# Attention weights in high and low parts for every second part of a row, and the output weights loaded in the mLSTM

## The chip, the core and the metric

The kernel runs on one core of a Trainium2 chip. Its engines are TensorE (PE, whose weight loads the profile lists apart as PEld), VectorE (DVE), ScalarE (ACT), GpSimd (POOL) and SyncE (SP), which here only issues DMAs. Each engine takes its instructions in order and waits for others by semaphores. The metric is the device time of one execution in microseconds.

## What is computed

One step of a one-layer encoder, for a prompt of 2048 tokens and a sample of 32 tokens with a past of 1024. Half of the mixing width is an mLSTM of 4 heads, half stick-breaking attention of 8 heads of 64; both go through one output projection, and a gated feed-forward net with a short convolution follows. The stages run one after the other: front (norm, input projection), attention, mLSTM, output projection, feed-forward up, feed-forward down.

```python
def stick_breaking_block(q, k, v, q_pos, k_pos):
    z = jnp.einsum('bhtd,bhsd->bhts', q, k).astype(jnp.float32) * (SB_DIM ** -0.5)
    mask = k_pos[None, :] < q_pos[:, None]
    log_beta = jnp.where(mask, jax.nn.log_sigmoid(z), -jnp.inf)
    log_1m = jnp.where(mask, jax.nn.log_sigmoid(-z), 0.0)
    rest = lax.cumsum(log_1m, axis=3, reverse=True) - log_1m
    a = jnp.exp(log_beta + rest)
    return jnp.einsum('bhts,bhsd->bhtd', a.astype(v.dtype), v)
...
    mix = jnp.concatenate([y_a, y_b], axis=-1) @ p['w_out']
    x = x + g1 * mix
```

## The kernel before

**Attention.** A row is a head h and a query block i of 128 tokens. It is cut into parts of up to four key blocks, last part first; such a part is an item (h, i, g), and a head has 40 of them: four rows of one item, four of two, four of three, four of four. In all there are 320 items of the prompt, 6 of the sample (ahead of head 3) and 10 that only turn past keys and queries. An item goes through the engines like this:

- PE multiplies queries and keys into a_z (L973; a mask product, L984, for a row's first item), which has NZ = 3 buffers. It waits there until ACT's second sigmoid of the item three before is done.
- ACT makes sigmoid(-z) into aB (L894) and sigmoid(z) into aS (L899, ring of 8).
- DVE runs the product along the row backwards into aC (L919).
- POOL multiplies aS by it (L957): these are the weights.
- PE turns them, 128 columns at a time, into a_x (L999, NX = 2 buffers).
- ACT (even items) or DVE (odd items) copies them into aA (L903, L886, ring of 4).
- PE multiplies weights and values in float32, one product of 128x64 a key block (L1015).
- DVE copies a finished row from a_out into aof (L934, ring of RO = 8), and SP stores it (L846).

The order is written out by hand: each engine walks `steps` and at step n does the operation for an item at a fixed distance (PE turns n-3, makes z of n+4 and the product of n-6; ACT makes the sigmoids of n+2, then copies n-4; DVE scans n, copies n-4, finishes n-7). So whoever waits holds up everything behind it on its engine.

SP loads queries and keys of head h+1 (six DMAs, L810) and its values (L828, av, two buffers) when the first row of head h is done, ahead of the store of that row; the loads of heads 0 and 1 stand at the start. In head 3 it also loads the whole of w_out (4 MB, L864), into the memory that the turned past keys have left.

**mLSTM.** A loop over 17 tiles of 128 tokens. SP loads ahead (three parts of the projections, a slice of w_ada for the modulation); ACT and POOL split w_out into high and low parts of the rounded format beside tiles 0 and 1 (L1141, L1128), four slices of 128x1024 each. The 16-record product of the modulation (L1266) closes each tile on PE.

**Output projection.** Per tile: loads (L1376 to L1378), norms on ACT and DVE, a turn on PE, a split of y, then three products each of 128x512 for (high, high), (low, high) and (high, low).

## Time and profile before

| | us |
|---|---|
| median of 3 runs (lowest, highest) | 3372.08 (3371.84, 3379.27) |
| the profiled execution | 3376.13 |
| its span on the core | 3374.5 |
| PE busy in it | 3177.0 (94%) |
| PEld, DVE, ACT, POOL busy | 2801.5, 1541.5, 1074.6, 757.8 |

Busy times are shares of the whole span and average over stages with different limits; which stage is bound by what is read from stretches of it. Attention lies between about 806 and 1345 us, the mLSTM from there to 1540, the output projection from 1540 to about 1778.

### The profile page before, as it was taken

The numbers are of one execution on the slowest core, as the hardware profiler recorded it, in microseconds if no ns is written. First come the engines' busy times: TensorE is split into PE (matmuls) and PEld (weight loads), VectorE is DVE, ScalarE is ACT, GpSimd is POOL, SyncE is SP. The second block draws the span as 40 slices with busy tenths as digits, with TensorE's granted clock in tenths as the row PEclk, the third lists the DMA queues.
The fourth block names the chain that finished last, engine by engine and source line by source line (L and its number), as shares of the span: only waits on it lengthen the run. The fifth ranks groups of instructions, "written<-read, shape, count | busy, mean of one in ns | idle before, by whom it ended". The sixth has DMA issues, their size and how long they took to land. (4 is left out here: it accounts for less than half of the span.)

```text
span 3374.5 us, 45756 instructions
## 1 busy us (share of the span) xinstructions
PE 3177.0 (94%) x17258; PEld 2801.5 (83%) x17258; DVE 1541.5 (46%) x1982; ACT 1074.6 (32%) x2063; POOL 757.8 (22%) x669
## 2 busy tenths in 40 slices
PE   7999998998999999896996999999999994999999
PEld 3878887777998998675886999999999994887886
DVE  1300025513887898674653544444344434234322
ACT  3611122213766776223553222122212212112111
POOL 3411113212665665200111111111111112002000
PEclk9999999998999999898997999999999997999999
DMA  5322224424423420564644111111111114335332
GB/s 185 113 67 69 75 79 129 137 90 118 112 52 101 95 56 12 187 217 146 194 150 150 51 50 50 50 34 42 50 50 50 50 38 152 140 121 174 139 136 70
DMA packets 249431, 335.88 MB, mean 100 GB/s; under 512 B 58380, under 2 KB 170440, under 8 KB 242508
## 3 DMA queue, kind: packets, MB, share of 16 engines
q1 hardware_dynamic: 233102, 284.75, 27.6%
q0 software_dynamic: 14864, 49.31, 4.3%
q8 instruction: 82, 1.34, 0.2%
q14 instruction: 51, 0.42, 0.0%
q10 hardware_dynamic: 1332, 0.06, 0.0%
HBM read 225.16 MB, written 108.89 MB: 99 GB/s over the span
## 5 line engine op out<-in xcount | busy, mean ns | idle before, releaser
L1774 PE MATMUL facc<-h2H,fwH 128*128 128x416 f32 x1760 | 617.5, 351 | 25.5 <-DVE h2L L1723 25.5
L1774 PE MATMUL facc<-h2L,fwH 128*128 128x416 f32 x1760 | 617.1, 351 | 0.0
L1774 PE MATMUL facc<-h2H,fwL 128*128 128x416 f32 x1760 | 617.0, 351 | 0.0
L642 PE MATMUL pacc<-pring,h1H 128*128 128x512 f32 x1360 | 444.3, 397 | 10.6 <-POOL h1L L524 5.8
L957 POOL TENSOR_TENSOR aS<-aS,aC 128x512 f32<-128x512 f32 (+3 forms) x326 | 333.7, 1029 | 203.1 <-DVE aC L919 200.3
L919 DVE TENSOR_TENSOR_SCAN aC<-aB,aC,a 128x512 f32<-128x512 f32 (+3 forms) x326 | 362.8, 1113 | 16.1 <-ACT aB L894 9.9
L1666 ACT ACTIVATE fU<-facc 128x416 f32<-128x416 f32 (+1 forms) x220 | 113.1, 514 | 787.5 <-PE facc L1774 787.5
L1740 DVE TENSOR_SCALAR fV<-fU,fcw,fcb 128x2048 f32<-128x2048 f32 x88 | 110.2, 1295 | 536.8 <-ACT fU L1668 536.7
L1774 PEld LDWEIGHTS facc<-h2H,fwH 128*128 128x128 f32 x1760 | 330.9, 188 | 28.8 <-issue 26.2
L1774 PEld LDWEIGHTS facc<-h2L,fwH 128*128 128x128 f32 x1760 | 331.0, 188 | 2.4
L1774 PEld LDWEIGHTS facc<-h2H,fwL 128*128 128x128 f32 x1760 | 330.8, 188 | 2.6
L1983 PE MATMUL dacc<-dwH,daH 128*128 128x512 f32 (+1 forms) x748 | 294.2, 393 | 37.0 <-POOL dwL L1850 24.5
L1710 POOL TENSOR_TENSOR fwL<-fraw,fwH 128x1024 fp32r<-128x1024 f32 x44 | 132.4, 3011 | 848.2 <-ACT fwH L1657 848.2
L642 PEld LDWEIGHTS pacc<-pring,h1H 128*128 128x128 f32 x1360 | 259.2, 191 | 66.2 <-POOL pring L520 6.9
L1015 PEld LDWEIGHTS a_out<-av,aA 128*128 128x128 f32 x2176 | 283.5, 192 | 19.3 <-issue 1.9
L1983 PE MATMUL dacc<-dwL,daH 128*128 128x512 f32 (+1 forms) x748 | 293.6, 393 | 0.0
L1983 PE MATMUL dacc<-dwH,daL 128*128 128x512 f32 (+1 forms) x748 | 293.6, 392 | 0.0
L1015 PE MATMUL a_out<-av,aA 128*128 128x64 f32 x2176 | 284.4, 270 | 0.0
L642 PE MATMUL pacc<-pring,h1L 128*128 128x512 f32 x680 | 267.6, 394 | 0.0
L973 PE MATMUL a_z<-ak,aq 128*128 128x512 f32 (+3 forms) x640 | 210.6, 411 | 13.2 <-DMA aq<-qk_T 13.2
L1923 ACT ACTIVATE daH<-da 128x2816 fp32r<-128x2816 f32 (+1 forms) x34 | 83.5, 2456 | 406.2 <-PE dacc L1983 350.3
L894 ACT ACTIVATE aB<-a_z 128x512 f32<-128x512 f32 (+3 forms) x326 | 174.4, 535 | 118.0 <-PE a_z L984 50.7
(261 smaller groups left out, 4773.7 us busy)
## 6 DMA issues: line engine op xcount, KB each, us to landing
da<-act_d SPq DMA_DIRECT2D x32, 1408.0 KB, 7.8
proj_out<-pstage SPq DMA_DIRECT2D x119, 256.0 KB, 2.0
fraw<-w_up SPq DMA_DIRECT2D x44, 512.0 KB, 5.7
act_d<-fV SPq DMA_DIRECT2D x22, 1024.0 KB, 5.3
qk_T<-pturn POOLq DMA_DIRECT2D x68, 256.0 KB, 3.1
mwa<-w_ada SPq DMA_DIRECT2D x16, 1024.0 KB, 5.4
praw<-w_in SPq DMA_DIRECT2D x56, 256.0 KB, 2.9
aq<-qk_T SPq DMA_DIRECT2D x28, 512.0 KB, 11.8
```

The lines of the kernel that those rows point to most:

```text
L642: op = mm_(acc[:, n % NB], h[:, kk, tok(t)], weight(q, w), start=(kk == 0 and part == 0), stop=(kk == KD - 1 and part == 2))
L894: nc.scalar.activation(part(B, RB, n), part(Z, NZ, n), ACT.Sigmoid, scale=-1.0).then_inc(pass_ready, 1)
L919: v.tensor_tensor_scan(buf[:, a:b][:, ::-1], part(B, RB, n)[:, ::-1], nought[:, 0:width(n)], buf[:, b:b + 1], ALU.mult, ALU.add).then_inc( ...
L957: nc.gpsimd.tensor_tensor(at, at, buf[:, a + 1:b + 1], ALU.mult).then_inc(w_ready, 1)
L973: mm = nc.tensor.matmul(to, Q[:, b, half, i * P:(i + 1) * P], K[:, b, span], start=(half == 0), stop=(half == 1), skip_group_check=True)
L1015: mm = nc.tensor.matmul(O[:, r % 2, 0:SD if kind == PROMPT else 4 * SD], weight[:, j * P:(j + 1) * P], value, start=(top(n) and j == 0), s ...
L1666: op = nc.scalar.activation(U[:, j, 2 + at:2 + end], acc[:, bank(q, w), 0:end - at], ACT.Copy)
L1710: nc.gpsimd.tensor_tensor(wL[:, j], raw[:, j], wH[:, j].bitcast(F32), ALU.subtract).then_inc(w_low, 1)
L1740: v.tensor_scalar(V[:, j, at:at + width], U[:, j, u0:u0 + width], tap(0), cb[:, ft], ALU.mult, ALU.add).then_inc(first_tap, 1)
L1774: mm = nc.tensor.matmul(dst, a[:, j, kk], h[:, kk, cols], start=(kk == 0 and m == 0), stop=(kk == KD - 1 and m == 2))
L1923: nc.scalar.activation(aH[:, i.b, :, 0:i.width], a[:, i.b, :, 0:i.width], ACT.Copy).then_inc(a_high, 1)
L1983: mm = nc.tensor.matmul(acc[0:w, i.b], l[:, i.b, kk, 0:w], m[:, kk], start=(kk == 0 and n == 0), stop=(kk == NF - 1 and n == 2))
```

## The change

1. Every second item of the prompt (the 160 of `in_two`, on 608 of the 1088 key blocks) is weighed in two parts. ACT copies the turned weights into AH, in the rounded format F32R; DVE subtracts that from a_x into AL. PE multiplies AH by the pair [high part, low part] of the values (128 columns), then AL by the high part (64 columns), both into the same row of a_out. DVE copies 128 columns of such a row into aot, and POOL adds the two halves nine items later (`add_parts`), before SP may store the row. 112 rows of 128 are of that kind.
2. ACT now copies every turned item, the others into A as before, and does so at the beginning of its step, ahead of the two sigmoids. DVE copies only the turned past keys. Each of the rings is two deep.
3. The values of head h+1 are split (ACT `split_values`, POOL a subtraction) at item (h, 8, 2), the thirteenth of head h; those of head 0 at its third item. ACT waits there for the load of these values.
4. The ring of finished rows, aof, is 4 deep, not 8.
5. w_out is loaded at the end of SP's list in the mLSTM instead of in head 3, and split at the start of the output projection: ACT all eight slices, POOL and DVE four subtractions each. The gate and norm rows are loaded ahead of the first tile there. The bias of the modulation has a buffer of its own.

```diff
+    in_two = set([n for n in scored if items[n][0] == PROMPT][1::2])
...
+    split_at = {scored[2]: 0}
+    split_at.update({items.index((PROMPT, h, NPT // 2, NPT // 2 // W4)): h + 1 for h in range(SH - 1)})
-    NZ, NX, RB, RS, RA, RC, RO = 3, 2, 4, 8, 4, 4, 8
+    NZ, NX, RB, RS, RA, RC, RO = 3, 2, 4, 8, 2, 4, 4
+    RT = 4
...
                 sp.wait_ge(o_taken, r + 1)
+                if r in rows_in_two:
+                    sp.wait_ge(o_summed, rows_in_two.index(r) + 1)
...
-                if kind == PROMPT and (h, i) == (3, 0):
-                    sp.wait_ge(turned, max(x for x in range(N) if items[x][0] in (KEYS, QUERIES)) + 1)
-                    sp.wait_ge(blank_stored, 16)
-                    sp.dma_start(w_out[:], d["w_out"].rearrange("(k p) n -> p k n", p=P)).then_inc(w_out_in, 16)
...
+                ring, order, done = (AH, two, high_ready) if n in in_two else (A, whole, taken[0])
+                if order[n] >= RA:
+                    act.wait_ge(av_done, rank[kept_by[n]] + 1)
+                to = ring[:, order[n] % RA, 0:width(n)]
+                nc.scalar.activation(to, X[:, n % NX, 0:width(n)], ACT.Copy).then_inc(done, 1)
...
+            def split_values(h):
+                b = h % 2
+                act.wait_ge(v_in[b], 16 * (h // 2 + 1))
+                nc.scalar.activation(V2[:, b, :, 0], V[:, b], ACT.Copy).then_inc(v_high, 1)
             for n in steps:
+                every(take, n - 4)
+                if n in split_at:
+                    split_values(split_at[n])
                 scores(passing, n + 2)
                 scores(stopping, n + 2)
-                every(take_even, n - 4)
...
+                elif n in in_two:
+                    dve.wait_ge(high_ready, two[n] + 1)
+                    at = two[n] % RA
+                    v.tensor_tensor(AL[:, at, 0:width(n)], X[:, n % NX, 0:width(n)], AH[:, at, 0:width(n)].bitcast(F32),
+                                    ALU.subtract).then_inc(taken[1], 1)
...
+            BEHIND = 9
+
+            def add_parts(n):
+                if not last(n) or row(n) not in rows_in_two:
+                    return
+                e, p = rows_in_two.index(row(n)), prompt_row(n)
+                pool.wait_ge(o_taken, row(n) + 1)
+                at_least(pool, stored[p % RO], 16 * (p // RO))
+                nc.gpsimd.tensor_tensor(of[:, p % RO], ot[:, e % RT, 0:SD], ot[:, e % RT, SD:], ALU.add).then_inc(o_summed, 1)
             for m, n in enumerate(scored):
...
                 nc.gpsimd.tensor_tensor(at, at, buf[:, a + 1:b + 1], ALU.mult).then_inc(w_ready, 1)
+                if n in split_at:
+                    e = split_at[n] % 2
+                    pool.wait_ge(v_high, split_at[n] + 1)
+                    nc.gpsimd.tensor_tensor(V2[:, e, :, 1], V[:, e], V2[:, e, :, 0].bitcast(F32), ALU.subtract
+                                            ).then_inc(v_low, 1)
+                if m >= BEHIND:
+                    add_parts(scored[m - BEHIND])
...
+                    if n in in_two:
+                        nc.tensor.matmul(out[:, 0:2 * SD], AH[:, two[n] % RA, cols],
+                                         V2[:, h % 2, b].rearrange("p s e -> p (s e)"), start=first, stop=False,
+                                         skip_group_check=True)
+                        mm = nc.tensor.matmul(out[:, 0:SD], AL[:, two[n] % RA, cols], V2[:, h % 2, b, 0], start=False,
+                                              stop=end, skip_group_check=True)
...
             tiles(sp, body)
+            sp.dma_start(w_out[:], d["w_out"].rearrange("(k p) n -> p k n", p=P)).then_inc(w_out_in, 16)
+            sp.wait_ge(w_out_in, 16)
             sp.wait_ge(mod_row, NPT)
```

How the rows of an engine stand is shown at three places. First ACT in head 5, where it comes to the ninth item (384 wide). Before:

```order
L894 ACTIVATE aB<-a_z 128x128
L899 ACTIVATE aS<-a_z 128x128
L903 ACTIVATE aA<-a_x 128x256
L894 ACTIVATE aB<-a_z 128x512
L899 ACTIVATE aS<-a_z 128x512
L894 ACTIVATE aB<-a_z 128x512
L899 ACTIVATE aS<-a_z 128x512
L903 ACTIVATE aA<-a_x 128x384
L894 ACTIVATE aB<-a_z 128x256
```

The same stretch after; `av<-av 128x16x64` is the split of the values of head 6, and aAH the high part of a_x:

```order
L917 ACTIVATE aA<-a_x 128x256
L890 ACTIVATE aB<-a_z 128x128
L895 ACTIVATE aS<-a_z 128x128
L917 ACTIVATE aAH<-a_x 128x512
L890 ACTIVATE aB<-a_z 128x512
L895 ACTIVATE aS<-a_z 128x512
L917 ACTIVATE aA<-a_x 128x384
L927 ACTIVATE av<-av 128x16x64
L890 ACTIVATE aB<-a_z 128x512
L895 ACTIVATE aS<-a_z 128x512
L917 ACTIVATE aAH<-a_x 128x512
```

The copy has moved ahead of the sigmoids of its step, there is one in each step, and the split stands between the copy of the ninth item and the sigmoids of the fifteenth.

Second POOL at the start of head 5, after; `aS<-aS,aC` is the product of L957, `aof<-aot` the addition of a row's two halves, of which the one behind the width of 384 belongs to the last row of head 4:

```order
L1006 TENSOR_TENSOR aS<-aS,aC 128x512
L1006 TENSOR_TENSOR aS<-aS,aC 128x256
L1006 TENSOR_TENSOR aS<-aS,aC 128x512
L1006 TENSOR_TENSOR aS<-aS,aC 128x384
L1000 TENSOR_TENSOR aof<-aot 128x64
L1006 TENSOR_TENSOR aS<-aS,aC 128x512 x2
L1000 TENSOR_TENSOR aof<-aot 128x64
L1006 TENSOR_TENSOR aS<-aS,aC 128x512
L1006 TENSOR_TENSOR aS<-aS,aC 128x128
L1010 TENSOR_TENSOR av<-av 128x16x64
L1000 TENSOR_TENSOR aof<-aot 128x64
```

Before, POOL's list holds only the products here. Third SP at the start of the output projection, before:

```order
L1376 DMA ey<-h_d 128x512
L1377 DMA ey<-o_rows 128x512
L1378 DMA eo<-proj_out 128x512
L1389 DMA ewrow<-y_norms 128x1024
L1376 DMA ey<-h_d 128x512
```

And after:

```order
L1448 DMA egate<-mods 128x1024 x2
L1449 DMA ewrow<-y_norms 128x1024
L1453 DMA ey<-h_d 128x512
L1454 DMA ey<-o_rows 128x512
L1455 DMA eo<-proj_out 128x512
```

The gate (twice 512 KB) and the norm row (512 KB) now stand ahead of the first tile.

## Rows read from the trace of the kernel before

**Rows 1.** Busy time by stretch: stretch, its length, then each engine's busy us
```profile
core 0: us, PE busy (x) PEld busy (x) DVE busy (x) ACT busy (x) POOL busy (x), PEclk, DMA share, GB/s
806.00:1345.00 539.00, 524.20 (x4152) 496.46 (x4152) 460.24 (x624) 376.09 (x823) 333.74 (x326) 0.98 0.34 80
```

**Rows 2.** Timeline of PE at an item of one block: start us, us, line, records
```profile
1226.90 0.42 PE L973 MATMUL a_z<-ak,aq 128*128 128x128 f32 x2
1227.16 0.27 PE L984 MATMUL a_z<-ident_r,far_r 128*128 128x128 f32 x1
1227.27 0.83 PE L1015 MATMUL a_out<-av,aA 128*128 128x64 f32 x6
```

**Rows 3.** Groups by line in attention: busy us, mean ns, idle before
```profile
L894 ACT ACTIVATE aB<-a_z 128x512 f32<-128x512 f32 (+3 forms) x326 | 174.4, 535 | 118.0 <-PE a_z L984 50.7 <-PE a_z L973 45.9 <-DVE aC L919 12.9
L886 DVE COPY aA<-a_x 128x512 f32<-128x512 f32 (+2 forms) x163 | 103.1, 632 | 7.2 <-PE a_x L999 6.8
L903 ACT ACTIVATE aA<-a_x 128x512 f32<-128x512 f32 (+3 forms) x163 | 81.5, 500 | 48.8 <-PE a_x L999 48.4
```

**Rows 4.** Single lines: duration ns min/median/max, first and last start
```profile
L1141 ACT ACTIVATE w_out_high<-w_out_sb x8: 1040/1044/1056, 1351.0 to 1362.8; 128x1024 fp32r<-128x1024 f32 x8
...
L450 DVE TENSOR_TENSOR pturn<-pR,pturn x34: 685/692/693, 485.7 to 714.9; 128x512 fp32r<-128x512 f32 x34
```

**Rows 5.** Timeline of SP in heads 0 and 5: its DMA issues
```profile
821.94 0.59 SPq L828 DMA_DIRECT2D av<-proj_out  x1
...
1162.42 0.33 SPq L846 DMA_DIRECT2D o_rows<-aof  x1
1162.80 1.09 SPq L810 DMA_DIRECT2D ak<-qk_T  x2
...
1166.50 0.59 SPq L828 DMA_DIRECT2D av<-proj_out  x1
```

**Rows 6.** Landing of the values: issues of heads 1, 6 (KB, us), then all eight
```profile
av<-proj_out SPq DMA_DIRECT2D x1, 512.0 KB, 15.7
...
av<-proj_out SPq DMA_DIRECT2D x1, 512.0 KB, 15.6
...
DMA to landing us min/median/max: 5.9/15.6/16.4
```

**Rows 7.** Timeline of ACT in head 5, the copy of the ninth item
```profile
1169.55 0.50 ACT L903 ACTIVATE aA<-a_x 128x384 f32<-128x384 f32 x1
```

**Rows 8.** Timeline of PE, the product into a_z of the eighteenth item, heads 0, 5
```profile
828.14 0.71 PE L973 MATMUL a_z<-ak,aq 128*128 128x512 f32 x2
...
1172.26 0.71 PE L973 MATMUL a_z<-ak,aq 128*128 128x512 f32 x2
```

**Rows 9.** Timeline of POOL in head 5, the product of the ninth item
```profile
1165.29 0.87 POOL L957 TENSOR_TENSOR aS<-aS,aC 128x384 f32<-128x384 f32 x1 [0.36 <-DVE aC L919]
```

**Rows 10.** Head 3: SP's load, PE behind its gap, then a stretch with PEclk
```profile
1047.54 0.39 SPq L864 DMA_DIRECT2D w_out_sb<-w_out  x1
...
1064.68 1.09 PE L999 MATMUL a_x<-ident,aS 128*128 128x128 f32 x4 [6.89 <-DVE aA L886]
...
1065.00:1071.00 6.00, 6.00 (x27) 0.50 0.03 5
```

**Rows 11.** Timeline of the mLSTM's first tiles: DVE, POOL and PE's modulation
```profile
1373.97 10.21 DVE L1168 TENSOR_TENSOR mVU<-mVI,gate_cols 128x516 f32<-128x516 f32 x1
...
1374.37 9.25 POOL L1128 TENSOR_TENSOR w_out_low<-w_out_sb,w_out_high 128x1024 fp32r<-128x1024 f32 x4
...
1371.26 3.62 PE L1266 MATMUL mpm<-mwa,silu_c 128*2 128x256 f32 x16
1388.96 3.61 PE L1266 MATMUL mpm<-mwa,silu_c 128*2 128x256 f32 x16
1398.63 1.67 PE L1266 MATMUL mpm<-mwa,silu_c 128*2 128x256 f32 x7
```

**Rows 12.** Timeline of SP at the end of the mLSTM
```profile
1511.60 0.59 SPq L1099 DMA_DIRECT2D mRU<-ug_d  x1
...
1533.22 0.27 SPq L1107 DMA_DIRECT2D mods<-mmod_rows  x1
```

**Rows 13.** Start of the output projection: ACT's first operation, DMA from 1539 to 1553
```profile
1545.69 0.31 ACT L1423 ACTIVATE esq<-ey 128x128 f32<-128x128 f32 x1 [23.79 <-DMA eo<-proj_out]
...
DMA packets 1725, 3.96 MB, mean 283 GB/s; under 512 B 183, under 2 KB 183, under 8 KB 1725
```

More of the change, by code:

```diff
@@ L706, in _, with attention @@
                         turn_weights()
-def attention(k, c, w_out):
+def attention(k, c):
     nc, d = k.nc, k.d
@@ L729, in attention @@
     before = lambda h: sum(items[n][0] == SAMPLE or items[n][1] < h for n in scored if items[n][0] != SAMPLE or h > 3)
-    NZ, NX, RB, RS, RA, RC, RO = 3, 2, 4, 8, 4, 4, 8
+    in_two = set([n for n in scored if items[n][0] == PROMPT][1::2])
+    by_dve = [n for n in range(N) if n in in_two or items[n][0] == KEYS]
+    by_act = [n for n in range(N) if n not in by_dve]
+    two = {n: m for m, n in enumerate(sorted(in_two))}
+    whole = {n: m for m, n in enumerate(n for n in scored if n not in in_two)}
+    nth = {n: m for group in (by_act, by_dve) for m, n in enumerate(group)}
+    rows_in_two = sorted({row_of[rank[n]] for n in in_two})
+    split_at = {scored[2]: 0}
+    split_at.update({items.index((PROMPT, h, NPT // 2, NPT // 2 // W4)): h + 1 for h in range(SH - 1)})
+    NZ, NX, RB, RS, RA, RC, RO = 3, 2, 4, 8, 2, 4, 4
+    RT = 4
     qk_in = [k.sem("qk_loaded0"), k.sem("qk_loaded1")]
@@ L975, in z @@
                 else:
-                    for u in range(2):
-                        pe.wait_ge(taken[u], max(x for x in range(N) if items[x][0] in (KEYS, QUERIES) and x % 2 == u) // 2 + 1)
+                    for source in (KEYS, QUERIES):
+                        taken_to(pe, max(x for x in range(N) if items[x][0] == source))
                     at_least(pe, stop_ready, m - NZ + 1)
@@ L1011, in av @@
                         pe.wait_ge(v_in[h % 2], 16 * (h // 2 + 1))
-                weight = part(A, RA, n)
+                if n in in_two:
+                    pe.wait_ge(v_low, h + 1)
+                out = O[:, r % 2]
                 for j, b in enumerate(blocks(n)):
-                    value = V[:, h % 2, b] if kind == PROMPT else vs[:, b, h * 4 * SD:(h + 1) * 4 * SD]
-                    mm = nc.tensor.matmul(O[:, r % 2, 0:SD if kind == PROMPT else 4 * SD], weight[:, j * P:(j + 1) * P], value,
-                                          start=(top(n) and j == 0), stop=(g == 0 and j == len(blocks(n)) - 1),
-                                          skip_group_check=True)
+                    first, end = top(n) and j == 0, g == 0 and j == len(blocks(n)) - 1
+                    cols = slice(j * P, (j + 1) * P)
+                    if n in in_two:
+                        nc.tensor.matmul(out[:, 0:2 * SD], AH[:, two[n] % RA, cols],
[3 more added lines that the diff above has]
+                                              stop=end, skip_group_check=True)
+                    else:
+                        value = V[:, h % 2, b] if kind == PROMPT else vs[:, b, h * 4 * SD:(h + 1) * 4 * SD]
+                        mm = nc.tensor.matmul(out[:, 0:SD if kind == PROMPT else 4 * SD], A[:, whole[n] % RA, cols], value,
+                                              start=first, stop=end, skip_group_check=True)
                 mm.then_inc(av_done, 1)
@@ L1124, in body @@
             def body(t, u, r, first):
-                if isinstance(t, int) and t in (0, 1):
-                    for kk in range(t * KD // 2, (t + 1) * KD // 2):
-                        pool.wait_ge(o_high, kk + 1)
-                        nc.gpsimd.tensor_tensor(oL[:, kk], w_out[:, kk], oH[:, kk].bitcast(F32), ALU.subtract).then_inc(o_low, 1)
                 pool.wait_ge(h_ready, t + 1)
@@ L1138, in body @@
             def body(t, u, r, first):
-                if isinstance(t, int) and t in (0, 1):
-                    for kk in range(t * KD // 2, (t + 1) * KD // 2):
-                        nc.scalar.activation(oH[:, kk], w_out[:, kk], ACT.Copy).then_inc(o_high, 1)
                 act.wait_ge(qkv_in[u], 48 * r + 48)
@@ L1387, in slot @@
                     load(i.ahead(3))
[L1388 to L1390 removed]
+            for t in range(3):
                 load(Turn(t, t, 0))
[L1392 to L1394 removed]
             turns_of_four(sp, slot)
@@ L1398, in _ @@
         def _(pool):
+            for kk in range(0, KD, 2):
+                weights_split(pool, kk)
             def store(i):
@@ L1416, in _ @@
         def _(act):
+            for kk in range(KD):
+                nc.scalar.activation(wH[:, kk], raw[:, kk], ACT.Copy).then_inc(w_high, 1)
             def spread(i):
@@ L1474, in _ @@
             v = nc.vector
-            dve.wait_ge(rows_in, 16)
+            dve.wait_ge(rows_in, 48)
+            for kk in range(1, KD, 2):
+                weights_split(dve, kk)
             def norm(i):
@@ L1552, in slot @@
                     for kk in range(KD):
+                        if isinstance(i.t, int) and i.t == 0 and half == 0:
+                            pe.wait_ge(w_low[kk % 2], kk // 2 + 1)
                         for n, (a, w) in enumerate(((yH, wH), (yL, wH), (yH, wL))):
```

136 lines of the change are left out of this document (77 added, 59 removed).

## The prediction

> **What bounds the kernel now.** I read the views in this order. The page's chain of waits says little here, since it names only the last stage, so I went by stretches. Stick-breaking attention runs from about 806 to 1345 us, and in its 539 us PE is busy for 524 while DVE, ACT and POOL have 460, 376 and 334 [rows 1]. PE sets the pace, DVE is not far behind. The change therefore pays only if PE's work per block shrinks, and it costs wherever PE is made to wait. So I looked next at what one PE record takes there, and then at who would be late for PE at each wait that the change adds.
>
> **Part 1, the product itself: nothing gained.** A block of weights times values is today one float32 product, which the trace records as two loads and two matmuls. After an item of one block, six records end at 1227.27+0.83 = 1228.10, the record ahead ends at 1227.16+0.27 = 1227.43: 0.67/6 = 0.112 us each, 0.224 us a block [rows 2]. A block in two parts also has two records: 128 columns in the rounded format, then 64. What does a record of 128 rounded columns with 128 new weights cost? The same rows hold one: the pair into a_z ends at 1226.90+0.42 = 1227.32, the mask product behind it at 1227.43, 0.11 us later. So it is the load of 128 weights that sets 0.11 us, in either format, and the short matmuls hide behind it. Two records of 0.112 replace two of 0.112: 0 us over the 608 blocks in two parts. I take 0.
>
> The Trainium skill (TensorE: Matmul & The Clock Gate, Weight-path perf modes) says the compiler turns on a fast weight load for 128 weights whenever the input isn't FP32. If the rounded format counted as such, a record would cost its columns alone; the row of 0.11 us speaks against it. This is rival 2 below.
>
> **Part 2, what is added on ACT, DVE and POOL.** ACT now copies all of the roughly 326 turned items instead of half: 163 more at 0.50 us, 82 us of work, and eight splits of the values, at 1.04 us each as the equal-sized split of w_out [rows 3, 4]. Its three operations an item come to 0.535+0.534+0.50 = 1.57 us, against PE's 524/326 = 1.61 us an item [rows 1, 3]. DVE subtracts where it copied: 0.69 us for 128x512 by the like operation that leaves PSUM in the rounded format in the first stage, against 0.63 in the mean for the copy [rows 3, 4], 0.06 x 160 = 10 us, and some 7 us for output copies twice as wide in 112 rows, on 460. POOL gets 112 small additions of at most 0.4 us and eight subtractions of 9.25/4 = 2.3 us [rows 11]: 63 us on 334. In throughput PE stays the bound, with little room on two engines; between 0 and 30 us may be lost by coupling (5% of 539 plus the splits), and I take 8, because the in-order slack between turning an item and needing it is about two items.
>
> **Part 3, the new wait of ACT: the term that decides.** In the order after, ACT splits the values of head h+1 right behind its copy of the ninth item of head h (384 wide), before the two sigmoids of the fifteenth. That split waits until the values of head h+1 are in. Where is that load? In head 5, SP issues it at 1166.50 behind six loads of queries and keys that began at 1162.80 [rows 5]; it takes 15.6 us to land (5.9 in the first case; 15.6 in the median; 16.4 at most) [rows 6], so it lands at 1182.1. ACT is at that copy at 1169.55 today [rows 7]. It will stand in the split for over 12 us, with the sigmoids, the copies for PE and everything else in its order queued behind. PE can go on until its product into a_z for the eighteenth item, because a_z has three buffers and the one it needs is freed by the sigmoid of the fifteenth: that product starts at 1172.26 today [rows 8]. ACT frees it at 1182.1 + 1.04 (split) + 0.49 + 0.59 (two sigmoids, the first overlapped) + about 0.1 = 1184.3. PE loses 12.0 us.
>
> The load also starts later. SP's stores are in order, and the last row of head 4 is now stored only after POOL has added its parts, nine items further: after the 384-wide product of head 5, which ends at 1165.29+0.87 = 1166.16 [rows 9], plus 0.4 for the addition, where SP stored at 1162.42 [rows 5]. That is 4.1 us for the whole chain of loads. PE then loses 16.1 us in head 5. The same subtraction, whose rows stand here for heads 0 and 5 alone, gives in the other heads: head 0 has its load at 821.94 (15.7 us) and the product at 828.14 [rows 5, 6, 8], 11.7 us, with no store ahead; head 1 15.1, head 2 16.7, head 3 14.0 (the sample rows stand between store and load, so there is no delay), heads 4 and 6 16.2 and 16.6. Head 7 has no split. The sum of seven is 106 us. The shorter ring of finished rows (four, not eight) would by itself make POOL wait behind the same loads, but by the time POOL comes to that addition ACT's wait has outlasted them; it adds nothing.
>
> **The clock.** After PE has idled, this trace shows half clock: 6.89 us without work, then granted clock 0.50 for the next 6 us (the 1.2 GHz level) [rows 10], a loss of 3 us; each of the seven stalls is longer. I take 2.5 us each, 17 us, between 12 and 23.
>
> **Part 4, w_out leaves attention.** In head 3 SP issues the 4 MB load at 1047.54; the stores of that head's rows sit behind it, DVE waits for one, and PE idles 6.89 us before 1064.68 and then works at half clock [rows 10]: 6.9 + 3 = 10 us come back.
>
> **Part 5, mLSTM.** The split of w_out went beside its first tiles. DVE's product of 1373.97 takes 10.21 us instead of 0.69 while POOL runs four subtractions in 9.25 us, and the 16-record group of PE returns after 17.70 us (1371.26 to 1388.96) where the next comes after 9.67 [rows 11]. Removing the split gives 17.70 - 9.67 = 8.0 us. The load of w_out now follows SP's last tile, whose last issue is near 1511.6; SP needs it before 1533.22, where it stores the modulation [rows 12], 21.6 us later. In attention everything that stood behind the same 4 MB was through 17.1 us after its issue, when PE came back [rows 10], so it fits: 0.
>
> **Part 6, the start of the output projection.** The split stands here now: ACT eight times 1.04 = 8.3 us from about 1540 [rows 4], where its first square starts at 1545.69 today [rows 13], so 3 us late by that alone; and SP issues 1.5 MB of rows ahead of the first tile. The queue moved 3.96 MB between 1539 and 1553 [rows 13], with its first 2 us empty: 0.33 MB/us, so 1.5 MB are 4.5 us, of which about one passes while SP is still issuing. DVE's four subtractions (about 1.3 us each, twice the 0.69 of half the width less a start) wait for those rows and run beside POOL's four of 2.3. Between 3.4 us (the loads alone) and 6.5 (DVE starts its norm only when all four are done behind POOL's), I take 4.7.
>
> The Trainium skill (SBUF — State Buffer, SBUF: two separate sides) says that a VectorE operation with two SBUF inputs and GpSimd lock each other out for one whole instruction. The mLSTM's rows agree in kind, but DVE waited there through four of POOL's instructions, not one [rows 11]. By the rule as it stands DVE's four would wait for one at most, and the start would cost 3.4 to 4 us.
>
> **Sum.** 106 + 17 + 8 - 10 - 8 + 4.7 = +118 us. The profiled execution took 3376.1 us (span 3374.5), 4 us over the median of the runs, 3372.1; on the median that is 3490 us, 3.5% slower.
>
> **Rivals.**
> 1. *The loads are in when ACT asks.* This is the case that ends on the other side. The place is the same split; it decides at a landing time of about 5.7 us after issue (1166.50 to 1172.26). The first such load took 5.9 us with little ahead of it, so it isn't absurd; against it, the seven others took 15.5 to 16.4 us with the same six loads ahead, which the change leaves in place. Then 106 and 17 fall away: 3372 + 8 - 10 - 8 + 4.7 = 3367 us, within 0.3%. Chance 0.04, with 0.02 more for a version of it in which coupling costs nothing (3359, faster).
> 2. *The rounded format loads its weights faster.* Two records would cost about 0.12 us (0.06 is what the 128-column product takes behind a 512-column one) instead of 0.224: 608 x 0.10 = 61 us less, 3429 us, still slower, since the stalls stay. Chance 0.05.
> 3. *ACT or DVE becomes the bound between the stalls.* ACT's 1.57 us an item against 1.61 leaves 2%; if waits of DVE on ACT's high part cost a tenth of 539 us, 54 us instead of 8: 3536 us. Chance 0.09.
> 4. *The delay through POOL's additions is hidden*, 23 us less: 3467 us. Chance 0.08.
>
> **Chances and range.** The forecast 0.72. A measurement of this kernel tells about 0.3% (10 us) from no change. Faster 0.02, same 0.04, slower 0.94. For the forecast alone: clock 12 to 23, coupling 0 to 30, start of the projection 3.4 to 6.5, landing times by 0.4 x 7: 3476 to 3521. With rival 4 the range starts at 3459; rival 3's lower half takes it to 3525.
>
> **What would show it.** In the profile after: seven gaps of PE of 11 to 17 us, one a head but the last, ended by ACT; ACT idle before the split of the values, waiting for the DMA into av; granted clock 0.5 behind each. Matmuls of a_out at 0.11 us apart in both forms. No gap near 1057; the mLSTM's second tile as long as its third; the first product of the output projection 4 to 5 us later behind its stage's start. The forecast is wrong if av lands within 6 us of its issue, or if the records of the two-part blocks come closer than 0.1 us.

## The result and the profile after

The changed kernel takes 3512.91 us in the median of 4 runs (3505.70 to 3516.08), the kernel before 3373.22 on the same chip: a ratio of 1.0408, interval 1.0387 to 1.0428. That is 140 us more, inside the range of the forecast and 23 us above its value. The profiled execution has a span of 3512.1 us against 3374.5, 137.6 more.

Busy time by stretch, of attention, the mLSTM and the output projection, first of before, cut at PE's first and last records of each stage (columns as in [rows 1]):

```profile
core 0: us, PE busy (x) PEld busy (x) DVE busy (x) ACT busy (x) POOL busy (x), PEclk, DMA share, GB/s
806.53:1344.84 538.31, 524.20 (x4152) 496.46 (x4152) 460.12 (x623) 376.09 (x823) 333.74 (x326) 0.98 0.34 80
1344.84:1534.40 189.56, 170.07 (x1156) 128.47 (x1156) 128.22 (x238) 47.37 (x77) 31.92 (x29) 0.93 0.55 184
1534.40:1808.17 273.77, 219.11 (x1089) 184.82 (x1088) 138.26 (x226) 130.71 (x362) 28.68 (x36) 0.89 0.54 176
```

The same stretches of the changed kernel:

```profile
802.38:1480.40 678.02, 563.26 (x4152) 528.55 (x4152) 472.11 (x624) 447.35 (x990) 383.24 (x445) 0.88 0.26 57
1480.40:1661.68 181.28, 166.95 (x1156) 125.74 (x1156) 117.73 (x238) 39.80 (x69) 12.80 (x22) 0.95 0.64 217
1661.68:1940.94 279.26, 220.37 (x1088) 185.71 (x1088) 145.71 (x230) 138.44 (x370) 39.04 (x40) 0.89 0.53 172
```

Attention takes 139.7 us more, the mLSTM 8.3 less, the output projection 5.5 more. The rest differs by 0.7 us net: 4.2 less ahead of attention and 4.8 more behind the projection, where this change touches nothing; both move by as much between other executions of these kernels (attention starts between 801.1 and 807.7 us in the kept traces). PE has the same 4152 records in attention. Its idle time went from 14.1 (538.31 - 524.20) to 114.8 us, +100.7, and its busy time from 524.2 to 563.3, +39.1: the same number of records, done slower. Two causes are to be told apart, the waiting and the slowness.

The waits say who held PE. First what PE waited for in attention (us in total, times, longest), then ACT's wait at the split of the values:

```profile
PE a_z L1031 <- ACT aS L895: 101.0, 9, 16.8
PE a_x L1057 <- DVE aAL L957: 6.2, 13, 0.8
PE a_x L1057 <- ACT aA L917: 3.6, 5, 0.8
```
```profile
ACT av L927 <- DMA av<-proj_out: 104.4, 7, 17.3
```

Head 5 shows how it goes, in the timelines of SP, ACT and PE (start us, us, engine, line; in brackets the idle time before and who ended it). These rows answer to [rows 5, 7 and 8]:

```profile
1263.21 1.09 SPq L824 DMA_DIRECT2D ak<-qk_T  x2
1264.34 2.52 SPq L824 DMA_DIRECT2D aq<-qk_T  x4
1266.91 0.59 SPq L842 DMA_DIRECT2D av<-proj_out  x1
```
```profile
1265.75 0.51 ACT L917 ACTIVATE aA<-a_x 128x384 f32<-128x384 f32 x1
1282.32 1.06 ACT L927 ACTIVATE av<-av 128x1024 fp32r<-128x1024 f32 x1 [16.06 <-DMA av<-proj_out]
1283.28 0.58 ACT L890 ACTIVATE aB<-a_z 128x512 f32<-128x512 f32 x1
1283.76 0.59 ACT L895 ACTIVATE aS<-a_z 128x512 f32<-128x512 f32 x1
```
```profile
1268.23 0.61 PE L1057 MATMUL a_x<-ident,aS 128*128 128x128 f32 x4
1284.40 1.22 PE L1031 MATMUL a_z<-ak,aq 128*128 128x512 f32 x2 [15.56 <-ACT aS L895]
```

ACT is through with the ninth item at 1266.26, the values were issued at 1266.91 and land 15.4 us later; then come the split, the two sigmoids that free a_z, and PE. The product behind the gap takes 1.22 us where it took 0.71. The seven gaps are 10.9, 12.8, 15.9, 12.6, 16.8, 15.6 and 15.7 us, 100.2 in sum.

### The profile page after: what moved, and what is told of

It is laid out like the page before. It is cut to its first block and busy times, and to the rows that moved or that the text cites. A ratio compares the mean times of both kernels' runs of the same rounds, so it can differ in the third digit from the quotient of the medians.

```text
span 3512.1 us, 46398 instructions
## 1 busy us (share of the span) xinstructions
PE 3214.8 (92%) x17258; PEld 2832.9 (81%) x17258; DVE 1549.8 (44%) x1987; ACT 1146.6 (33%) x2230; POOL 799.9 (23%) x785
## 5 line engine op out<-in xcount | busy, mean ns | idle before, releaser
L1856 PEld LDWEIGHTS facc<-h2H,fwH 128*128 128x128 f32 x1760 | 331.2, 188 | 28.6 <-issue 26.1
L1031 PE MATMUL a_z<-ak,aq 128*128 128x512 f32 (+3 forms) x640 | 222.6, 432 | 114.3 <-ACT aS L895 101.0
L1031 PEld LDWEIGHTS a_z<-ak,aq 128*128 128x128 f32 x640 | 105.6, 207 | 118.2 <-ACT aS L895 103.9
L1057 PE MATMUL a_x<-ident,aS 128*128 128x128 f32 x1106 | 190.6, 290 | 11.2 <-DVE aAL L957 6.2
L2065 PEld LDWEIGHTS dacc<-dwH,daH 128*128 128x128 f32 (+1 forms) x748 | 138.8, 186 | 75.0 <-issue 41.1
```

The costliest lines, as they stand in the source:

```text
L1031: mm = nc.tensor.matmul(to, Q[:, b, half, i * P:(i + 1) * P], K[:, b, span], start=(half == 0), stop=(half == 1), skip_group_check=True)
L1057: mm = nc.tensor.transpose(X[:, n % NX, j * P:(j + 1) * P], src[:, j * P:(j + 1) * P], c["ident"][:])
L1856: mm = nc.tensor.matmul(dst, a[:, j, kk], h[:, kk, cols], start=(kk == 0 and m == 0), stop=(kk == KD - 1 and m == 2))
L2065: mm = nc.tensor.matmul(acc[0:w, i.b], l[:, i.b, kk, 0:w], m[:, kk], start=(kk == 0 and n == 0), stop=(kk == NF - 1 and n == 2))
```

## The experiments

Attention is measured as above, from PE's first product into a_z to its last record of the stage. Gaps are PE's idle times of over 1 us in it, after the first items. The times are medians; the ratio is against the kernel before on the same chip.

### The split of the values moved to the end of the head

```diff
-    split_at.update({items.index((PROMPT, h, NPT // 2, NPT // 2 // W4)): h + 1 for h in range(SH - 1)})
+    split_at.update({items.index((PROMPT, h, NPT - 1, 0)): h + 1 for h in range(SH - 1)})
```

> The changed kernel (3512.9 us), with the split of the next head's values moved from the ninth item's copy to the last item of the head, where those values have long landed. Theory (ACT's wait for the values is what costs): the seven gaps of PE ended by ACT, 100 us in sum, are gone, and the half clock behind them, 33 us; that alone gives 3380. But the ring of finished rows is four deep: POOL's addition of the fifth row must wait until the first row's store, which stands behind seven loads, has landed, some 11 us after POOL's turn, of which 4 to 5 us are slack. So I expect gaps of 4 to 10 us a head ended by POOL, 50 us in sum with the later start of the loads, and half clock behind some: 3430 to 3450. Rival 1 (the ring costs nothing, as a slack of four rows suffices): 3370 to 3390. Rival 2 (the cost is throughput of ACT and DVE, not the wait): above 3480.

3449.21 us, ratio 1.0208 (1.0183 to 1.0232). ACT's wait is gone, and another has come in its place, as the waits of PE and of POOL show:

```profile
PE a_x L1057 <- POOL aS L1006: 43.9, 7, 8.0
```
```profile
POOL aof L1000 <- DMA o_rows<-aof: 66.1, 6, 12.0
```

POOL may not overwrite the ring of four finished rows before the first row's store has landed, and that store stands behind the seven loads: SP is held for 11.5 to 13.7 us in issuing it, where it needs 0.3 us for another store. Seven gaps, 1.4 to 8.0 us, 43.9 in sum where 50 were expected. But PE's busy time did not fall with the gaps in the profiled execution:

```profile
807.66:1428.51 620.85, 563.27 (x4152) 529.14 (x4152) 472.02 (x624) 448.29 (x990) 381.72 (x445) 0.91 0.28 62
```

563.27 us as in the changed kernel, for less than half its gaps. This execution was the longest of the four (3461.98 us, against 3433.69 to 3449.47), so the half clock probably cost less in the others, some 23 us in one of median length if the difference is all the clock's (an estimate: 563.27 - 527.73, less 3461.98 - 3449.21; 527.73 us is PE's busy time without gaps, from the next run).

### The same with a ring of eight rows, and the ring of eight alone

```diff
-    NZ, NX, RB, RS, RA, RC, RO = 3, 2, 4, 8, 2, 4, 4
+    NZ, NX, RB, RS, RA, RC, RO = 3, 2, 4, 7, 2, 4, 8
```

> As the one with the late split, and the ring of finished rows eight deep again (the ring of ACT's second sigmoids seven deep instead of eight, to make room for it). What is left of the change in attention is then the two-part product, ACT's and DVE's added work and POOL's additions. Theory: no gap of PE over 3 us after the first items, attention 531 to 545 us where it had 538 before; with the mLSTM's -8 and the projection's +5.6 us 3365 to 3380. Rival 1 (ACT or DVE is the bound between the stalls): attention 560 us or more, 3395 and up. Rival 2 (the ring cost nothing): the same time as with the late split alone.

> The changed kernel with the ring of finished rows eight deep (the ring of second sigmoids seven deep for room), the split where the change put it. Theory: ACT's wait outlasts the wait of POOL for the first row's store, so the ring adds nothing: 3505 to 3518, the seven gaps still ended by ACT and within 0.5 us of 10.9, 12.8, 15.9, 12.6, 16.8, 15.6, 15.7. Rival (part of the gaps is the ring's): some gaps shorter by 2 us or more, 3500 or less.

With the late split and the ring of eight 3377.77 us, ratio 1.0011 (1.0001 to 1.0020): both waits are gone, no gap over 1 us is left, and so is the slowness of PE:

```profile
805.47:1347.79 542.32, 527.73 (x4152) 496.68 (x4152) 469.56 (x624) 447.10 (x990) 382.54 (x445) 0.99 0.32 71
```

The ring of eight alone, with the split where the change put it (the ring of second sigmoids again seven deep): 3506.57 us, ratio 1.0398 (1.0380 to 1.0415), PE's wait for ACT 102.5 us in place of 101.0:

```profile
PE a_z L1031 <- ACT aS L895: 102.5, 9, 17.3
```

The gaps stand, six of them within 0.5 us of before and the one in head 2 1.3 us longer. So the ring adds nothing as long as ACT waits, and it is what is late next when ACT doesn't: two waits behind the same loads, of which only the longer is seen.

### The loads ahead of the last row's store; the values ahead of queries and keys

The first edit, in SP's loop over the rows:

```diff
-                if kind == PROMPT and i == 0 and 0 < h < SH - 1:
-                    load(h + 1)
+                if kind == PROMPT and i == NPT - 1 and h < SH - 2:
+                    load(h + 2)
                 store(scored[m])
```

> The changed kernel with the loads for head h+1 issued ahead of the store of the last row of head h-1, so that they no longer wait for POOL to add that row's parts. Theory: in heads 1, 2, 4, 5 and 6 the values land some 4.6 us earlier, 23 us in sum, and in head 3, where the sample's rows stood in between, they land before ACT asks, so its gap of 12.6 us and the half clock behind it (3 us) go too: 3513 - 23 - 16 = 3474, some 3 to 6 us less if the half clock shortens with the gaps. Rival (the delay through POOL is hidden, the loads are limited by other transfers): 3495 to 3513, heads 1, 2, 4, 5 and 6 unchanged.

3455.56 us, ratio 1.0250 (1.0232 to 1.0269), 57 us less than the changed kernel where 39 were expected. The gaps are 10.7, 4.8, 10.1, none in head 3, 8.8, 8.6 and 9.0 us. In heads 1, 2, 4, 5 and 6 they shrank by 6 to 8 us, 35 in sum, where 23 were expected. That does not make POOL's delay larger than expected, since the edit takes away more than the delay. Counted from the end of ACT's copy of the ninth item in head 5, SP issued the values 3.5 us earlier than that in the kernel before, 0.7 us later in the changed kernel, and 6.4 us earlier here (SP's row, then ACT's):

```profile
1218.21 0.59 SPq L842 DMA_DIRECT2D av<-proj_out  x1
```
```profile
1224.11 0.51 ACT L917 ACTIVATE aA<-a_x 128x384 f32<-128x384 f32 x1
```

In sum over the five heads the change delayed the issue by 22 us, as expected, and the edit brought it forward by 36, 14 us beyond where it had stood. So the late start of the loads was real and of the expected size.

The second edit, in `load`:

```diff
-                    at_least(sp, z_ready, before(h - 1))
+                    at_least(sp, av_done, before(h - 1))
+                    load_values(h)
                     load_part(h, slice(0, SEQ), qk_in[b])
-                    at_least(sp, av_done, before(h - 1))
-                load_values(h)
                 if h == 0:
+                    load_values(h)
```

> The changed kernel with the load of a head's values issued ahead of the six loads of its queries and keys. The first load of values, which had little ahead of it, took 5.2 to 5.9 us. Theory: the values are issued 3.7 us earlier and land some 6 us after issue instead of 15.6, 13.4 us earlier in all, so ACT's gaps shrink from 10.9, 12.8, 15.9, 12.6, 16.8, 15.6, 15.7 to about 0, 0, 2.5, 0, 3.4, 2.2, 2.3, 10 us in sum. Then the ring of four rows is what is late next: POOL waits for the first row's store behind the same seven loads, so the time is as with the late split, 3430 to 3450, and no less. Rival 1 (the ring costs nothing): 3385 to 3395. Rival 2 (a load's time is its own, not that of the loads ahead): gaps shrink by 3.7 us each, 3480.

3448.85 us, ratio 1.0217 (1.0201 to 1.0232), inside the expected range. This edit stands alone, without the one above. The values now land after 5.1 us, against 15.5 in the changed kernel, as the summaries of this DMA show (first the changed kernel, then this one):

```profile
DMA to landing us min/median/max: 5.2/15.5/16.6
```
```profile
DMA to landing us min/median/max: 4.3/5.1/7.4
```

The 15 us were the six transfers ahead, not the transfer's own. ACT's waits have nearly gone (they still leave PE gaps of 4.1, 0.8, 1.9 and 0.8 us in heads 2, 4, 5 and 6), and the ring of four takes over:

```profile
PE a_x L1057 <- POOL aS L1006: 25.9, 5, 6.7
PE a_z L1031 <- ACT aS L895: 8.2, 6, 4.1
```

### Both orders of the loads, with the ring of eight

This kernel has the two edits above and the ring of eight; the split stays at the ninth item.

> The changed kernel with its split where the change put it, but the loads for head h+1 issued ahead of the last row's store of head h-1, the values first among them, and the ring of finished rows eight deep (second sigmoids seven deep). Theory: the values are issued some 10 us earlier than in the changed kernel and land about 6 us later, before ACT asks in every head, and POOL waits for no store: no gap of PE over 3 us, 3370 to 3385, as with the late split and the ring of eight. Rival (a load that lands late has another cause than its place, or the waits move to the queries and keys): gaps of 3 us or more with half clock behind them, 3400 or more.

3378.63 us, ratio 1.0013 (1.0003 to 1.0022), attention 542.1 us, no gap over 1 us. Two different remedies, the split later or the load earlier, end at the same time, which leaves the waits, with the slow PE behind them, as the cause of all but 14 us of what attention lost.

### PE kept busy in the gaps

```diff
+            FILL = {n + 5: cnt for n, cnt in zip(split_items, (96, 113, 142, 111, 150, 139, 140))}
...
+                    if n in FILL:
+                        at_least(pe, o_taken, row(n - 10) - 1)
+                    for _ in range(FILL.get(n, 0)):
+                        nc.tensor.matmul(O[:, row(n - 10) % 2, 2 * P:], Q[:, b, 0, 0:P], K[:, b, 0:2 * P], start=True, stop=True,
+                                         skip_group_check=True)
                     at_least(pe, stop_ready, m - NZ + 1)
```

> The changed kernel with products of 128x256 that nobody reads, issued by PE in each of the seven gaps ahead of the product into a_z (96, 113, 142, 111, 150, 139 and 140 of them, at 0.11 us each about as long as the gap). The waits stay as they are; only PE does not idle in them. Theory (the half clock behind the gaps comes from the idling, and is worth 33 us of the change): granted clock 1.0 behind the gaps, 3513 - 33 = 3480, between 3475 and 3487. Rival 1 (the half clock has another reason): 3513. Rival 2 (the clock is full but the items behind a gap are held by ACT, DVE and POOL anyway, so that the slow PE was hidden): full clock and 3500 or more.

The products go to columns of a row's bank that nothing reads, but the sum in the bank's other columns is open then and does not seem to survive them: this kernel's first output is off by 0.22 (relative error). It serves for its time alone, which depends on no value. 3489.08 us, ratio 1.0346 (1.0330 to 1.0361), 24 us less with ACT's waits as long as before:

```profile
ACT av L927 <- DMA av<-proj_out: 106.7, 7, 17.4
```
```profile
804.74:1453.82 649.08, 634.05 (x5043) 603.17 (x5043) 469.76 (x624) 446.11 (x990) 382.62 (x445) 0.99 0.27 60
```

The mean granted clock of attention is 0.99 instead of 0.88. The 891 added products take 106.9 us, counted from the end of the record ahead of each of the seven groups to the end of its last product. Without them 649.08 - 106.9 = 542.2 us of attention are left, as in the kernels without gaps (542.3). They are 6 to 7 us longer than the gaps they fill, which is enough to put the time 2 us above the expected range. Attention fell by 28.9 us, and with those 6 to 7 us by some 35. The half clock came from the idling, and in this pair of executions it was worth 35 us.

### The low product left out

```diff
-                        nc.tensor.matmul(out[:, 0:2 * SD], AH[:, two[n] % RA, cols],
-                                         V2[:, h % 2, b].rearrange("p s e -> p (s e)"), start=first, stop=False,
-                                         skip_group_check=True)
-                        mm = nc.tensor.matmul(out[:, 0:SD], AL[:, two[n] % RA, cols], V2[:, h % 2, b, 0], start=False,
-                                              stop=end, skip_group_check=True)
+                        mm = nc.tensor.matmul(out[:, 0:2 * SD], AH[:, two[n] % RA, cols],
+                                              V2[:, h % 2, b].rearrange("p s e -> p (s e)"), start=first, stop=end,
+                                              skip_group_check=True)
```

> As the kernel with the late split and the ring of eight, with the 608 products of the low part of the weights left out (so the output lacks their share); all copies, subtractions and waits stay. Theory (a record costs its 128-weight load, 0.112 us, whatever its format and its 64 or 128 columns): PE has 608 x 0.112 = 68 us less to do, 460 us of work in attention; then DVE with 470 us and ACT with 447 are next, each in order, so attention takes 480 to 510 us instead of 542 and the whole 3315 to 3345. Rival 1 (the rounded format's weights load faster, 0.06 us): 36 us less, 3342, with PE still the busiest. Rival 2 (ACT and DVE already bind at 542): 3370 or more.

3343.50 us, ratio 0.9910 (0.9893 to 0.9927); attention 507.8 us, 34.5 less than with the late split and the ring of eight:

```profile
804.06:1311.84 507.78, 472.40 (x3544) 433.56 (x3544) 463.97 (x624) 441.31 (x990) 382.32 (x445) 0.98 0.34 76
```

The time alone would also fit a faster load of rounded weights (3342). The trace decides: over the 448 pairs of neighbouring records of the high part the second starts 0.111 us (median) behind the first. So a record costs its 0.11 us. PE's busy time falls by 55 us, 13 less than the 68 expected, which was not explained, and its idle time rises by 21 us, in pieces of under 1.1 us (35.4 us where 14.6 were), with DVE at 464 of 508 us and ACT at 441 the nearest reasons; that they are the reason is argued and no run tested it. Whatever holds PE does so near 508, not at 542.

### The move of w_out alone

The kernel before with the past keys in a buffer of their own, and w_out loaded and split as after.

> The kernel before with the move of w_out alone: attention as before (the past keys in memory of their own), w_out loaded at the end of the mLSTM and split at the start of the output projection, whose gate and norm rows come ahead of its first tile. Theory: -6.9 us for the gap in head 3 and -3 for the half clock behind it, -8.3 in the mLSTM and +5.6 in the output projection, as the two traces have them: 3373 - 12.6 = 3360. Rival (head 3 loses as much without the load, since the six other loads and the store behind them stay): 3370.

3359.46 us, ratio 0.9961 (0.9948 to 0.9975): faster than both kernels. Head 3 has no gap, and attention is 10.4 us shorter than before:

```profile
805.96:1333.92 527.96, 521.11 (x4152) 493.71 (x4152) 459.82 (x623) 375.82 (x823) 333.74 (x326) 0.99 0.33 73
```

### The start of the output projection, twice

First the rows of gate and norm behind the first tile, as before the change, with DVE's subtractions ahead of its wait for them:

```diff
-            dve.wait_ge(rows_in, 48)
             for kk in range(1, KD, 2):
                 weights_split(dve, kk)
+            dve.wait_ge(rows_in, 16)
```

In SP's list, which is not shown, the norm row goes behind the first tile again and the gate behind the third, as before the change.

> As the kernel before with w_out moved, but in the output projection the first tile is loaded ahead of the norm row and the gate, as before the change, and DVE's four subtractions do not wait for these rows. Theory (about 4 us of the projection's later start is the 1.5 MB ahead of the first tile, the rest the splitting itself): 3360 - 4 = 3356. Rival (ACT's eight slices, 8.3 us, and the subtractions set the start): the same as with w_out moved, within 1 us.

3358.63 us, ratio 0.9952 (0.9938 to 0.9966), not to be told from the 3359.46: the rival holds. Counted from the mLSTM's last product, DVE starts its four subtractions after 7.2 us instead of 12.5, but they take 12.4 us instead of 7.6, so that it is through with them after 19.7 us instead of 20.1. First with w_out moved, then with the rows later, and POOL's four there:

```profile
1527.94 7.59 DVE L1370 TENSOR_TENSOR ewL<-w_out_sb,ewH 128x1024 fp32r<-128x1024 f32 x4 [11.88 <-DMA ewrow<-y_norms]
```
```profile
1521.40 12.41 DVE L1371 TENSOR_TENSOR ewL<-w_out_sb,ewH 128x1024 fp32r<-128x1024 f32 x4 [6.59 <-ACT ewH L1424]
...
1520.50 12.22 POOL L1371 TENSOR_TENSOR ewL<-w_out_sb,ewH 128x1024 fp32r<-128x1024 f32 x4 [7.54 <-ACT ewH L1424]
```

Then all eight subtractions to POOL:

```diff
-            (nc.gpsimd if kk % 2 == 0 else nc.vector).tensor_tensor(
+            nc.gpsimd.tensor_tensor(
```

> As the kernel with the rows later, and POOL makes all eight subtractions of w_out, DVE none. With the rows later DVE's four took 12.41 us beside POOL's 12.22, where one of DVE's took 1.21 alone and one of POOL's 2.34: they slow each other, and DVE comes to its first norm 3.0 us after it could (1533.73 instead of some 1530.7). Theory: the first product of the output projection comes 2 to 3 us earlier (28.3 to 29.3 us behind the last product of the mLSTM instead of 31.3), and POOL's eight end after some 19 us, before PE needs the last of them: 3355 to 3357. Rival (DVE's norm is slowed by POOL's subtractions beside it as much as its own subtractions were): 3358 to 3360, first product at 31 us or later.

3365.54 us, ratio 0.9981 (0.9972 to 0.9990): worse than theory and rival. The first product comes 35.5 us behind the mLSTM's last, 4.2 later than with the rows later. DVE does begin its norm early, and then each of its operations waits:

```profile
1529.76 1.68 DVE L1493 TENSOR_TENSOR ey<-ey,est 128x512 f32<-128x512 f32 x1
1531.47 2.72 DVE L1495 TENSOR_TENSOR ey<-ey,ewrow 128x512 f32<-128x512 f32 x1
1534.12 2.82 DVE L1496 SCALAR_TENSOR_TENSOR ey<-ey,est,ewrow 128x512 f32<-128x512 f32 x1
1536.87 2.82 DVE L1499 TENSOR_TENSOR ey<-ey,eo 128x512 f32<-128x512 f32 x1
...
1544.16 0.69 DVE L1493 TENSOR_TENSOR ey<-ey,est 128x512 f32<-128x512 f32 x1
1544.89 0.69 DVE L1495 TENSOR_TENSOR ey<-ey,ewrow 128x512 f32<-128x512 f32 x1
1545.50 0.74 DVE L1496 SCALAR_TENSOR_TENSOR ey<-ey,est,ewrow 128x512 f32<-128x512 f32 x1
1546.16 0.68 DVE L1499 TENSOR_TENSOR ey<-ey,eo 128x512 f32<-128x512 f32 x1
```
```profile
1519.31 19.83 POOL L1371 TENSOR_TENSOR ewL<-w_out_sb,ewH 128x1024 fp32r<-128x1024 f32 x8 [7.54 <-ACT ewH L1424]
```

The same four operations take 0.68 to 0.74 us once POOL is through. Beside it the first takes 1.68 and the others 2.7 to 2.8, some 2 us more each, which is most of one of POOL's instructions (19.83/8 = 2.5 us).

## Why the prediction was right, and which term was too small

The forecast was the likeliest case, the mechanism is the one that it named, and the experiments take it apart with the same result. Term by term, where "measured" is from the traces as said:

| term | predicted | measured | by |
|---|---|---|---|
| product in two parts | 0 | about 0 | starts of the records, below |
| seven waits of ACT | 106 | 100.2 | the seven gaps |
| half clock behind them | 17 (12 to 23) | 35.5 | busy time, 563.26 - 527.73 (with the ring of eight alone 28.6) |
| coupling of ACT, DVE and PE | 8 (0 to 30) | 14.4 | attention, 542.32 - 527.96 |
| w_out out of head 3 | -10 | -10.4 | attention, 527.96 - 538.31 |
| split of w_out out of the mLSTM, with the load at its end | -8 | -8.3 | the stretch |
| start of the projection | +4.7 | +5.5 | the stretch |
| sum | +118 | +137 | span, +137.6 |

The forecast was 23 us low. The sum stayed in its range although the clock's term left its own, because room had been kept for coupling, which took only part of it; that is luck as far as the clock goes. The bounds of the single terms also add to 3473 to 3523 us, where the prediction says 3476 to 3521, and how it came to 3459 and 3525 for the wider range it doesn't show; the measured 3512.91 lies inside by either.

**The step that failed** is the clock's: "6.89 us without work, then granted clock 0.50 for the next 6 us ... I take 2.5 us each, 17 us, between 12 and 23" [rows 10]. I took one gap as the measure of seven. The gaps cost 5 us each in the mean, because the clock stayed at half for longer than behind that one, and not for a length that the gap tells. Behind the gap of 15.9 us in head 2 of the changed kernel it took 18 us to come back:

```profile
1006.60:1012.00 5.40, 5.40 (x23) 5.22 (x24) 3.86 (x6) 4.03 (x9) 4.67 (x6) 0.50 0.06 14
1012.00:1018.00 6.00, 6.00 (x27) 5.61 (x27) 3.79 (x5) 2.62 (x6) 2.46 (x3) 0.50 0.03 5
1018.00:1024.00 6.00, 6.00 (x28) 5.61 (x27) 2.32 (x5) 2.94 (x6) 1.90 (x3) 0.50 0.03 8
1024.00:1030.00 6.00, 6.00 (x48) 5.68 (x46) 5.02 (x6) 4.74 (x11) 4.31 (x5) 0.94 0.03 7
```

Behind 12.6 us in head 3 it was some 7 us, and with the late split 27 us behind a gap of only 8.0. The clock's 18.5 us and the coupling's 6.4 that were missing, less the 6 by which the waits were too high, are the 19 between the two sums.

**The waits**, the term that decides, were 6 us too high. The subtraction by issue, landing and PE's turn held within 0.9 us in five heads; in heads 1 and 3 it was 2.3 and 1.4 us too high. That the ring "adds nothing" was right, and the ring of eight shows it. That 23 us of the waits came from the later start of the loads was right too: from the kernel before to the changed one the issue moved back by 22 us against ACT's copy, in the five heads concerned. The run with the loads first took away 35, but it also moved the loads 14 us ahead of where they had been.

**The product** was costed from one row at 0.224 us a block [rows 2]; after, a two-part block in head 5 has the records of its high part at 1262.87, 1263.10 and 1263.32, 0.22 to 0.23 us apart:

```profile
1262.87 0.31 PE L1077 MATMUL a_out<-av,aAH 128*128 128x128 f32 x1
1263.02 0.25 PE L1080 MATMUL a_out<-av,aAL 128*128 128x64 f32 x1
1263.10 0.31 PE L1077 MATMUL a_out<-av,aAH 128*128 128x128 f32 x1
1263.24 0.25 PE L1080 MATMUL a_out<-av,aAL 128*128 128x64 f32 x1
1263.32 0.31 PE L1077 MATMUL a_out<-av,aAH 128*128 128x128 f32 x1
```

The starts alternate, 0.15 us and then 0.08, so the prediction's sign "closer than 0.1 us" was badly put; it is the pair that tells, and it costs what it did. Rival 2 (rounded weights load faster) falls with that. The Trainium skill (TensorE: Matmul & The Clock Gate, Weight-path perf modes) has 128 weights load fast whenever they are not FP32. The rounded format gains nothing of the kind here: 0.111 us a record of 128 columns with another of its kind behind it, 0.112 us one of 64 columns in float32.

**Coupling**, as I call what is left of attention's loss without the waits, was 14.4 us: PE's idle time rose by 7.7 (14.59 against 6.85 us) and its busy time by 6.6 beyond the kernel with w_out moved alone (the ring of second sigmoids was seven deep in the first of the two). Rival 3, with 54 us, was too dark, but without the low product attention still takes 508 us, which is how near the next bound is. The added work was priced a little high: 90, 17 and 63 us on ACT, DVE and POOL, where 71, 12 and 50 were measured in attention. What of the 6.6 is pacing by the other engines and what the longer records wasn't separated.

**The start of the projection** was sized well for half a reason. The first product comes 31.2 us behind the mLSTM's last where it came after 26.8, 4.4 later, as forecast. But the rows ahead of the first tile are only one of two things that hold DVE: with them behind it, nothing is gained that can be told from no change (0.8 us), since DVE's subtractions then run beside all four of POOL's, and the two hold each other up. In the prediction this was the upper end of the term, and should have stood beside the loads as its second half. How much either costs by itself no run shows.

**Rival 1** was priced at a landing time of 5.7 us, which is too generous. By the prediction's own subtraction the split and the two sigmoids take 2.2 us more, so that the values would have to land 3.5 us after an issue where it was, and ahead of the issue where the change put it. The run with the values first bears this out: they land after 5.1 us in the median and PE still has gaps that ACT ends. With the ring of eight as well, and either the split late or the loads early and the values first among them, the change comes to 3378 us, 0.1% more than before.

That figure holds two parts that cancel. The move of w_out alone takes 0.4% off the kernel before; the two-part product and its work, on top of that and without a single long wait, put 0.5% on again. So the two-part product gains nothing and costs some 14 us of attention, and the fastest complete kernels here are those that keep the old product and only move w_out.

## What to carry to other kernels

A wait put into the middle of an engine's hand-written order is priced by the landing time of what it waits for, less the moment at which the bound engine needs the next thing behind it; read the landing time with the transfers ahead of it, since their place in the queue, not the size, made 15 us out of 5. When one such wait is removed, look for the second that stands behind the same transfers (here a ring too short by four rows) before counting the gain. Price idle time of PE above its length: here 100 us of gaps cost 35 more at half clock, and in another run 32 us of gaps cost 37.

## What the runs showed of the hardware

- **Half clock does not follow the length of the gap.** In the profiled executions, PE's busy time above the 527.73 us without gaps was 35.5 us for gaps of 100.2 us in sum (the changed kernel), 28.6 for 101.7 (the ring of eight alone), 29.3 for 52.1 (the loads first), 35.5 for 43.9 (the late split, in the longest of its four executions) and 37.1 for 31.9 (the values first). After single gaps of 12.6, 15.9 and 8.0 us the half clock lasted 7, 18 and 27 us, although PE was busy without a break in it. Repeated runs spread as well: 3433.69 to 3461.98 us with the late split, a spread of 28 us, against 3372.20 to 3382.31 for 13 runs of the kernel before on the same chip. What decides the length stays open.
- **VectorE and GpSimd hold each other up** when both read two operands from SBUF: DVE's 0.68 to 0.74 us became 2.7 to 2.8, beside GpSimd instructions of 2.5 us in the mean, and four subtractions of 1.21 us beside four of 2.34 took 12.4 us; all eight together took 13.3 (1520.50 to 1533.81), nearly the sum of their times alone (14.2). This agrees with the Trainium skill (SBUF — State Buffer, SBUF: two separate sides), a lock for one whole instruction, which [rows 11] alone did not: there one DVE operation took 10.21 us beside four of POOL's.
- **A queue's place is most of a load's time**: 512 KB landed after 5.1 us when first and 15.5 us when seventh (medians). The next in line pays at its issue: SP is held for 11.6 to 13.9 us in issuing the store behind the seven loads of the changed kernel, where another store takes 0.3 us.
